# Norm factors worked out on token columns, and two weight tiles taken together while the input is made

## What is computed

```
def rmsnorm(x, g):
    y = x * lax.rsqrt(jnp.mean(x * x, axis=-1, keepdims=True) + RMS_EPS)
    return y * g
def layer_norm(x, g, b):
    mu, var = mean of x, mean of (x - mu)^2 over channels
    return (x - mu) * lax.rsqrt(var + LN_EPS) * g + b
...
    f_l = modulate(rmsnorm(h_lat, norm2[i]), sh2_l, sc2_l)        # x * (1 + scale) + shift
    h_lat = h_lat + g2_l * peer(f_l, peer_wq[i], ...)
    return rmsnorm(h_lat, final_norm)
...
    h_l = xl * (1.0 + sc1_l) + sh1_l                              # second block, layer i
    o_l, o_c = even_mixer(h_l, h_c, ...)                          # i = 0; odd_mixer for i = 1
    xl = layer_norm(ALPHA * xl + gt1_l * o_l, ln1_g[i], ln1_b[i])
    h_l = xl * (1.0 + sc2_l) + sh2_l
    f_l = conv_ffn(h_l, w_gate[i], w_up[i], conv_w[i], conv_b[i], w_down[i])
    xl = layer_norm(ALPHA * xl + gt2_l * f_l, ln2_g[i], ln2_b[i])
```

## Time and profile before

| | us |
|---|---|
| median of 3 runs | 4767.77 (4763.95 to 4772.82) |
| the profiled execution, own time | 4765.72 |
| its span, first to last instruction | 4763.8 |
| TensorE busy | 4363.6 (92%) |
| VectorE busy | 2498.6 (52%) |
| GpSimd busy | 1804.2 (38%) |
| mean granted clock of TensorE | 0.959 |

### The profile page before, as it was taken

One profiled execution on the slowest core, in us unless ns is written; L12 is line 12 of the kernel. 1 busy time (PEld: TensorE's weight loads), 2 busy tenths in 40 slices (PEclk: granted clock), 3 DMA queues, 4 the chain that ended last, 5 costly groups with the idle time before them and its releaser, 6 DMA issues.

```text
span 4763.8 us, 51427 instructions
## 1 busy us (share of the span) xinstructions
PE 4363.6 (92%) x20890; PEld 3398.6 (71%) x20890; DVE 2498.6 (52%) x4227; ACT 1510.1 (32%) x2528; POOL 1804.2 (38%) x987
## 2 busy tenths in 40 slices
PE   7878999987779999999999989997999979988998
PEld 3667755456667888888888866675888857656886
DVE  4675745359868676664544342544344350364334
ACT  3212211034863232323222233543222232353232
POOL 2244423024965444444444413002223315333442
PEclk9998999989889999999999989998999989998999
DMA  5200300321355555454533310001212112102331
GB/s 216 81 27 6 117 27 27 133 85 49 128 199 187 171 172 173 155 177 163 181 129 133 116 62 15 19 19 40 67 63 67 63 31 62 36 1 71 97 93 49
DMA packets 170761, 441.31 MB, mean 93 GB/s; under 512 B 12220, under 2 KB 78972, under 8 KB 167581
## 3 DMA queue, kind: packets, MB, share of 16 engines
q1 hardware_dynamic: 168060, 422.61, 26.1%
q0 software_dynamic: 2464, 15.41, 0.8%
HBM read 402.32 MB, written 35.65 MB: 92 GB/s over the span
## 4 chain that ended last, share of the span: by engine, by line
PE 69%; DVE 6%; POOL 4%; ACT 3%; issue 2%; DMA 0%; POOLq 0%; ACTq 0%; DVEq 0%
PE psum L256 19%; PE psum L254 19%; PE psum L255 19%; PE psum L260 11%; POOL o L1600 2%; PE psum L281 1%; DVE o L1493 1%; POOL Pe L2411 1%; POOL Pd L2413 1%; DVE X L1882 1%; DVE ffl L1822 0%; DVE o L1495 0%; DVE rstd L1862 0%; DVE X L1885 0%; DVE ci L1444 0%
## 5 line engine op out<-in xcount | busy, mean ns | idle before, releaser
L244 POOL TENSOR_TENSOR pair<-raw_ring,pair 128x1024 fp32r<-128x1024 f32 x502 | 1244.4, 2493 | 2010.6 <-ACT pair L236 2010.5
L236 ACT CAST pair<-raw_ring 128x1024 fp32r<-128x1024 f32 x502 | 510.9, 1047 | 368.8 <-PE psum L256 315.7
L254 PE MATMUL psum<-pfh,pair 128*128 128x512 f32 x1152 | 451.6, 392 | 27.6 <-POOL pair L244 26.8
L1675 DVE SCALAR_TENSOR_TENSOR h<-psum,mods,h 128x512 f32<-128x512 f32 x512 | 370.7, 748 | 162.5 <-PE psum L256 160.7
L255 PE MATMUL psum<-pfl,pair 128*128 128x512 f32 x1152 | 449.9, 391 | 0.0
L256 PE MATMUL psum<-pfh,pair 128*128 128x512 f32 x1152 | 449.7, 390 | 0.0
L254 PE MATMUL psum<-ffh,pair 128*128 128x512 f32 (+1 forms) x1056 | 375.8, 356 | 44.9 <-DVE ffl L1822 44.9
L254 PE MATMUL psum<-Ah,pair 128*128 128x512 f32 x1024 | 400.9, 391 | 9.7 <-DVE h L1675 4.9
L255 PE MATMUL psum<-Al,pair 128*128 128x512 f32 x1024 | 400.5, 391 | 0.0
L256 PE MATMUL psum<-Ah,pair 128*128 128x512 f32 x1024 | 400.3, 391 | 0.0
L256 PE MATMUL psum<-ffh,pair 128*128 128x512 f32 (+1 forms) x1056 | 377.7, 358 | 0.0
(11 more groups left out here) (569 smaller groups left out, 8959.6 us busy)
## 6 DMA issues: line engine op xcount, KB each, us to landing
raw_ring<-wmod SPq DMA_DIRECT2D x144, 512.0 KB, 4.7
raw_ring<-peeru SPq DMA_DIRECT2D x128, 512.0 KB, 4.4
raw_ring<-peerv SPq DMA_DIRECT2D x128, 512.0 KB, 3.7
gates<-stage SPq DMA_DIRECT2D x16, 2048.0 KB, 6.4
Gb<-gates SPq DMA_DIRECT2D x32, 1024.0 KB, 9.5
raw_ring<-win SPq DMA_DIRECT2D x48, 512.0 KB, 4.5
raw_ring<-wgate SPq DMA_DIRECT2D x44, 512.0 KB, 3.5
raw_ring<-wup SPq DMA_DIRECT2D x44, 512.0 KB, 3.6
```

Source lines behind the costliest of these rows:

```text
L236: ac.e.copy(self.pair(t)[0], k.R.of(t)).then_inc(*k.A.up("hi", t))
L244: po.e.tensor_tensor(lo, k.R.of(t), hi.bitcast(F), ALU.subtract).then_inc(*k.G.up("lo", t))
L254: e.matmul(out, w[0], x[0], start=first, stop=False, skip_group_check=True)
L1675: e.scalar_tensor_tensor(out=h[:, j, :], in0=B.of(("down", gi, j)), scalar=m[:, 40 + j, 0:1], in1=h[:, j, :], op0=ALU.mult, op1=ALU.add).t ...
```

## The change

1. **Token columns.** The sum over channels is made with the data as the stationary side and one moving column, so that 128 tokens land on 128 partitions in one PSUM column (`tensor_columns`): 12 such matmuls for an RMS norm, 6 or 4 for a layer norm. Eps, root and reciprocal are then taken of a tile of 128x4 or 128x6 (`vector_column`, `scalar_column`), and `tensor_along` spreads the factor over all partitions with the identity as moving side (`rb`, one PSUM bank for each segment).
2. **Gain and modulation put together.** gain x (1 + scale) and bias x (1 + scale) + shift are made ahead of time (`vector_gains`). VectorE multiplies by gain and by the factor straight from PSUM, ScalarE adds the bias and rounds to the high part in one instruction, VectorE makes the low part of (x + bias) - high. Tiles 2 and 5 (`SECONDS`) have their low part made on GpSimd, from a copy with the bias that ScalarE writes.
3. **The residual** for the next layer is made behind the input, by `vector_keep`, from a copy of the factor in SBUF; it replaces the multiplication by ALPHA.
4. **Sums on GpSimd.** For norm2 and n3 ScalarE squares each h tile as it is made and GpSimd adds tiles 0 to 5 (`pool_squares`). For the means GpSimd adds X tiles 0 to 5 (`pool_sum`), so three products stand in place of eight, all behind the last projection.
5. **The variance's matmuls** are 64 output rows wide, in halves of the bank by turns, with four buffers for squares; a column of ones at rows 0 and 64 (`sel`) adds the halves in step 1. ScalarE copies the sums out of PSUM for it.
6. **Two weight tiles together.** `project_abreast` takes the first two weight tiles of a stage (wq 0 and 1, abin 0 and 1, gate 0 and up 0, dqk 0 and 1): for each input tile it multiplies both. It waits for both tiles' splits and for all of their banks ahead of the first matmul. The scores of wq 0 and 1 both come behind wq 2, the rotations of dqk 0 and 1 behind both.
7. Small things: the weights' first splits stand ahead of the norm at norm2 and n3 (and GpSimd's at the others, ahead of tiles 2 and 5), two small instructions on `mods` stand ahead of the last h, the context's load is issued earlier, the last norm writes the output with one VectorE and one ScalarE instruction a tile.

```diff
+def project_abreast(k, pe, names, x, segs, each, among=(0, 1, 2, 3, 4, 5, 6, 7)):
+    for n in names:
+        pe.wait_ge(k.W.split(n))
+        for s in range(len(segs)):
+            k.B.take((n, s), 1, among)
+            pe.wait_ge(k.B.free((n, s)))
+    for q in range(8):
+        qs = slice(128 * q, 128 * q + 128)
+        pe.wait_ge(each(q))
+        for n in names:
+            hi, lo = k.W.pair(n)
+            for s, (a, b) in enumerate(segs):
+                i = trio(pe.e, k.B.of((n, s))[:, 0:b - a], (hi[:, qs], lo[:, qs]), x(q, s), q == 0, q == 7)
+                if q == 7:
+                    i.then_inc(*k.P.up(n, s))
+    for n in names:
+        k.P.name("used", n)
...
+SECONDS = (2, 5)
+def second_made(k, key, q):
+    return k.G.at(key, "f", q) if q in SECONDS else k.V.at(key, "f", q)
+def pool_seconds(k, po, key, n, tmp, fh, fl):
+    for j in SECONDS:
+        po.wait_ge(k.A.at(key, "g", j))
+        po.e.tensor_tensor(fl[j][:, 0:n], tmp[j % len(tmp)][:, 0:n], fh[j][:, 0:n].bitcast(F), ALU.subtract).then_inc(*k.G.up(key, "f", j))
...
+def tensor_columns(k, pe, key, sources, n, w, among=(0, 1, 2, 3, 4, 5, 6, 7)):
+    bank = k.B.take((key, "col"), 1, among)
+    pe.wait_ge(k.B.free((key, "col")))
+    for i2, (x, ready) in enumerate(sources):
+        for c in range(n):
+            pe.wait_ge(ready(c))
+            i = mm(pe.e, bank[:, c:c + 1], x[:, 128 * c:128 * c + 128], w, i2 == 0 and c == 0, i2 == len(sources) - 1)
+    i.then_inc(*k.P.up(key, "col"))
...
+def tensor_along(k, pe, key, segs, among=(0, 1, 2, 3, 4, 5, 6, 7)):
+    for s in range(len(segs)):
+        k.B.take((key, "rb", s), 1, among)
+        pe.wait_ge(k.B.free((key, "rb", s)))
+    for s, (a, b) in enumerate(segs):
+        bank = k.B.of((key, "rb", s))
+        pe.wait_ge(k.V.at(key, "r"))
+        for c in range(a // 128, b // 128):
+            i = mm(pe.e, bank[:, 128 * c - a:128 * c - a + 128], k.r8[:, c:c + 1].to_broadcast([128, 128]), k.sq["ident"])
+        i.then_inc(*k.P.up(key, "rb", s))
...
+def vector_column(k, dv, key, n, eps):
+    r = k.r8[:, 0:n]
+    dv.wait_ge(k.P.at(key, "col"))
+    dv.e.tensor_scalar(r, k.B.of((key, "col"))[:, 0:n], eps, None, ALU.add).then_inc(*k.V.up(key, "ms"))
+    k.B.over((key, "col"), k.V.now())
+    dv.wait_ge(k.A.at(key, "sqrt"))
+    dv.e.reciprocal(r, r).then_inc(*k.V.up(key, "r"))
...
+    pool_squares(k, po, "sq2", k.psum, k.psq)
     k.G.name("end", "out")
+def pool_squares(k, po, key, total, sq):
+    for j in range(1, 6):
+        po.wait_ge(k.A.at(key, j))
+        po.e.tensor_tensor(total, sq[0] if j == 1 else total, sq[j % 4], ALU.add).then_inc(*k.G.up(key, j))
+        po.wait_ge(k.G.now())
...
-    everyone(k, pe, "out")
-    bank = B.take("ms2")
-    pe.wait_ge(B.free("ms2"))
-    for j in range(8):
-        pe.wait_ge(A.at("sq2", j))
-        mm(e, bank, k.sq["m1024"], k.psq[j % 2], j == 0, j == 7).then_inc(*P.up("sq2", j))
+    tensor_columns(k, pe, "n2", squares(k, "sq2", k.psum, k.psq), 4, k.sq["m1024"][:, 0:1])
+    tensor_along(k, pe, "n2", SEG1)
     P.name("end", "norm2")
-    everyone(k, pe, "norm2")
...
-    for n in range(16):
+    project_abreast(k, pe, [("wq", n) for n in range(2)], k.px, SEG1, lambda q: second_made(k, "n2", q))
+    for n in range(2, 16):
         project(k, pe, ("wq", n), k.px, SEG1)
-        if n:
-            scores(n - 1)
+        if n == 2:
+            scores(0)
+        scores(n - 1)
...
+    W.hi(ac, ("wq", 0))
+    scalar_column(k, ac, "n2", 4)
...
+    W.lo(po, ("wq", 0))
+    pool_seconds(k, po, "n2", 512, k.pft, k.pfh, k.pfl)
...
+def vector_apply(k, dv, key, src, segs, tmp, fh, fl):
...
+    for j in range(10):
+        if j < 8:
+            x = tmp[j % 4]
+            dv.wait_ge(second_made(k, key, j - 4) if j > 3 else None)
+            for s, (a, b) in enumerate(segs):
+                dv.wait_ge(k.P.at(src, "rb", s))
+                e.scalar_tensor_tensor(out=x[:, a:b], in0=k.X[:, j, a:b], scalar=c.gain[s][:, j:j + 1], in1=k.B.of((src, "rb", s))[:, 0:b - a],
+                                       op0=ALU.mult, op1=ALU.mult).then_inc(*V.up())
+                if j == 7:
+                    k.B.over((src, "rb", s), V.now())
+            V.name(key, "x", j)
+        i = j - 2
+        if i < 0 or i in SECONDS:
+            continue
+        dv.wait_ge(k.A.at(key, "hi", i))
+        for s, (a, b) in enumerate(segs):
+            e.scalar_tensor_tensor(out=fl[i][:, a:b], in0=tmp[i % 4][:, a:b], scalar=c.bias[s][:, i:i + 1], in1=fh[i][:, a:b].bitcast(F),
+                                   op0=ALU.add, op1=ALU.subtract).then_inc(*V.up())
+        V.name(key, "f", i)
...
+def scalar_apply(k, ac, key, src, segs, tmp, fh):
+    e, A, c = ac.e, k.A, k.lnv[key]
     for j in range(8):
-        x = tmp[j % 2][:, 0:n]
-        ac.wait_ge(ready(j), k.V.at(key, "f", j - 2) if j > 1 else None)
+        x = tmp[j % 4]
+        ac.wait_ge(k.V.at(key, "x", j))
         for s, (a, b) in enumerate(segs):
-            e.activation(x[:, a:b], k.X[:, j, a:b], AF.Identity, scale=k.ones16[:, 8 * s + j:8 * s + j + 1], bias=m[:, j0 + j, s:s + 1]).then_inc(*A.up())
-        A.name(key, "x", j)
-        ac.wait_ge(A.now())
-        e.copy(fh[j][:, 0:n], x).then_inc(*A.up(key, "hi", j))
-def vector_affine(k, dv, key, segs, tmp, fh, fl):
-    n = segs[-1][1]
+            e.activation(fh[j][:, a:b], x[:, a:b], AF.Identity, bias=c.bias[s][:, j:j + 1]).then_inc(*A.up())
+        A.name(key, "hi", j)
+        if j in SECONDS:
+            ac.wait_ge(A.now())
+            for s, (a, b) in enumerate(segs):
+                e.activation(x[:, a:b], x[:, a:b], AF.Identity, bias=c.bias[s][:, j:j + 1]).then_inc(*A.up())
+            A.name(key, "g", j)
+    for s, (a, b) in enumerate(segs):
+        e.copy(k.rstd[:, a:b], k.B.of((src, "rb", s))[:, 0:b - a]).then_inc(*A.up(key, "rstd", s))
+        k.B.over((src, "rb", s), A.now())
...
+def vector_keep(k, dv, key, n):
+    e, V, c = dv.e, k.V, k.lnv[key]
+    dv.wait_ge(k.A.at(key, "rstd", (n - 1) // 512), V.now())
     for j in range(8):
...
+        x = k.X[:, j, 0:n]
+        e.scalar_tensor_tensor(out=x, in0=x, scalar=c.ga[:, j:j + 1], in1=k.rstd[:, 0:n], op0=ALU.mult, op1=ALU.mult).then_inc(*V.up())
+    dv.wait_ge(V.now())
+    for j in range(8):
+        x = k.X[:, j, 0:n]
+        e.tensor_scalar(x, x, c.ba[:, j:j + 1], None, ALU.add).then_inc(*V.up())
...
         bank = k.B.of((key, "mean", s))
-        pe.wait_ge(count(s), k.B.free((key, "mean", s)) if j == 0 else None)
-        i = mm(pe.e, bank[:, 0:b - a], k.sq["m1024"], k.X[:, j, a:b], j == 0, j == 7)
+        pe.wait_ge(ready(s), k.B.free((key, "mean", s)) if j == 5 else None)
+        x = total[:, a:b] if j == 5 else k.X[:, j, a:b]
+        i = mm(pe.e, bank[:, 0:b - a], k.sq["m1024"], x, j == 5, j == 7)
...
+    for s in range(len(segs)):
         k.B.take((key, "var", s), 1, SIX)
         pe.wait_ge(k.B.free((key, "var", s)))
     for j in range(8):
         pe.wait_ge(k.A.at(key, "sq", j))
         for s, (a, b) in enumerate(segs):
-            i = mm(pe.e, k.B.of((key, "var", s))[:, 0:b - a], k.sq["m1024"], sqt[j % 2][:, a:b], j == 0, j == 7)
+            h = slice(64 * ((j + s) % 2), 64 * ((j + s) % 2) + 64)
+            i = mm(pe.e, k.B.of((key, "var", s))[h, 0:b - a], k.sq["m1024"][:, 0:64], sqt[j % 4][:, a:b], j < 2, j > 5)
         i.then_inc(*k.P.up(key, "var", j))
-def vector_norm(k, dv, key, segs, last=None):
+    n = segs[-1][1] // 128
+    tensor_columns(k, pe, key, [(total, lambda c: k.A.at(key, "sums", c // 4))], n, k.sel, SIX)
+    tensor_along(k, pe, key, segs, SIX)
...
+    vector_column(k, dv, key, segs[-1][1] // 128, LN_EPS)
...
     for s, (a, b) in enumerate(segs):
-        ac.wait_ge(k.V.at(key, "var", s))
-        e.activation(k.rstd[:, a:b], k.rstd[:, a:b], AF.Sqrt).then_inc(*A.up(key, "sqrt", s))
...
+        ac.wait_ge(k.P.at(key, "var", 7))
+        e.copy(total[:, a:b], k.B.of((key, "var", s))[:, 0:b - a]).then_inc(*A.up(key, "sums", s))
+        k.B.over((key, "var", s), A.now())
+    scalar_column(k, ac, key, n // 128)
...
-        if j:
-            tensor_mean(k, pe, key, j - 1, segs, lambda s: k.V.at(key, "res", j - 1, s))
-    tensor_mean(k, pe, key, 7, segs, lambda s: k.V.at(key, "res", 7, s))
-    tensor_norm(k, pe, key, segs, sqt)
+    tensor_mean(k, pe, key, 5, segs, total, lambda s: k.G.at(key, "sum", 5))
+    for j in (6, 7):
+        tensor_mean(k, pe, key, j, segs, total, lambda s: k.V.at(key, "res", j, s))
...
-            project_in(k, pe, ("gate", i, j), fx, segs, None if j else (lambda q: V.at(key, "f", q)), EIGHT)
+            if j == 0:
+                project_abreast(k, pe, [("gate", i, j), ("up", i, j)], fx, segs, lambda q: second_made(k, key, q))
+                continue
+            project_in(k, pe, ("gate", i, j), fx, segs, None, EIGHT)
...
-    vector_affine_scale(k, dv, key, m, 24, segs, A.at("end", before))
```

(11 more changed lines are left out.)

313 lines of the change are left out of this document (179 added, 134 removed).

## The result

| | before | after |
|---|---|---|
| median | 4770.3 (4763.95 to 4777.06, 4 runs) | 4697.1 (4690.99 to 4698.38, 4 runs) |
| span of the profiled execution | 4763.8 | 4695.3 |
| TensorE busy | 4363.6 | 4353.1 |
| mean granted clock | 0.959 | 0.965 |

The ratio is 0.9844, with a 95% interval of 0.9827 to 0.9861. The change is faster by 73 us where I had forecast 111, and the time lies 2 us above the high end of my range, 4695. The spans differ by 68.5 us, so 42.5 us of the forecast are missing.

A forecast was written before the change was run, and what follows sets the result against it. TensorE, busy 92% of the span, was taken as the bound, losing time at six norm-to-projection places. Gains 19.6 + 20.1 + 16.1 + 29 + 16.9 + 9.3 = 111.0 us gave a median of 4657, range 4632 to 4695.

The forecast's parts named there:

- 5 res1, ff1: From res1's norm to ff1's second weight tile: first matmul 4347.9 against 4360.2, end 4361.5 against 4378.4; gain 16.9 us.
- 6 end: From ff1 through the last norm to the output: mean 4.4 us sooner, end 4754.5 against 4763.8; gain 9.3 us.
- B: Rival: the clock stays at 1.2 GHz through the two-tile stretches; +42 us, 4699; chance 14%, whole or in part.
- A: Rival: the variance's 64-row products don't pair, so it costs as many matmul slots as before; +10.6 us, 4668; chance 12%.
- C: Rival: VectorE and GpSimd contend at every place, two to three us each; +13 us, 4670; chance 14%.
- Place 4: From ff0's norm to dqk: no bank collision, kept residual costs nothing; rotation ends 3897.6 against 3926.8; gain 29 us, the largest.
- Place 2: From n3 to abin, the even block's input: first matmul 2794.6 against 2805.74, end 2813.4 against 2833.6; gain 20.1 us.
- Place 3: From res0 to ff0: TensorE waits for a bank the spread factor holds; gain 16.1 us, 28 without that wait.
- place 1: From norm2 to wq, the routing product: TensorE starts about 983.4, end 996.7 against 1016.3; gain 19.6 us.
- D: Rival: the bank wait at res0 to ff0 costs nothing, since the input ends last anyway; 12.7 us less, 4644; chance 12%.
- E: Rival: slower than before, with 1.2 GHz far into the dense projections; 239 us at the low clock eat the gain; 2%.
- F: Rival: the first weight tiles' splits arrive late, so the two tiles aren't abreast; about +33 us, 4690; chance 3%.

## Why the prediction was wrong

The missing 42.5 us, by the steps of the prediction. "Measured" is what each place gained between the work ahead of it and the end of its second weight tile, for places 2 and 4 the start of the third, since the small products of both tiles now lie between.

| place | forecast | measured | what failed |
|---|---|---|---|
| 1 norm2, wq | 19.6 | 20.3 | |
| 2 n3, abin | 20.1 | 13.9 | first matmul 2.5 later; both tiles' small products together, 3.2 |
| 3 res0, ff0 | 16.1 | 14.9 | size only |
| 4 ff0, dqk | 29 | 22.1 | the cover of the kept residual |
| 5 res1, ff1 | 16.9 | 16.0 | size only |
| 6 end | 9.3 | 10.6 | |
| dense stretches | 0 | -32 | no term for it |
| elsewhere | 0 | +3 | 2.9 before norm2; not looked into |

**The sum treated everything outside the six places as unchanged.** That is the step that failed most, three quarters of the gap. The matmuls were the same instructions in the same order, the diff didn't touch them, and I took their duration over from before. What moved them was the allocation of 64 and 576 bytes ahead of them. The shifted versions of both kernels show this, at +30 and -32 us (by spans -28). It accounts for 25 of the 31.8; most of the rest, 6.6, is ff0's 256-column matmuls, at 117.8 ns for 113.3, and that cause is open. The trace of before held a hint: the two blocks stand at different remainders there, and their matmuls start 226.7 and 228.9 ns apart. I hadn't compared them. In the range no case had a loss outside the places, so the time fell 2 us above its end. The high bound was also lower than its own cases add up to: B alone is 4657 + 42 = 4699, and A, C and half of B are 4702, where I wrote 4695. With these it would have held the time, but not by its mechanism: the largest loss is in none of its cases.

**Place 4, the residual: "lies behind ff0's first two tiles ... nothing".** I had costed this for ff0 and then took it for dqk too. At ff0, TensorE has 96 matmuls ahead that ask VectorE for nothing. At dqk the next thing is a rotation that wants ScalarE, which wants two tiny products of VectorE that stand behind the residual. My sentence on the cover that could fail (7 us at places 3 and 4) had the size and half of the place: 8.07 us at place 4, none at place 3. Moving the residual gave back 9.4, and 7 in the end.

**Place 2: first matmul at 12.5 us after the last h.** It came after 15.05. I had taken "VectorE now also makes the affine part" as a cost per tile, and not read that three of them, and six products, stand ahead of the first low part in its order, nor that GpSimd's low part of tile 2 collides with it (2.18 for 0.94). The other order gave back 3.4 to 4.2. The second tile's end is 3.1 us later than forecast, so at the forecast's own mark the place gained 17.1. Another 3.2 go before the third tile starts, seen in the trace and not tried by itself: TensorE waits 2.82 us for the copies and squares of both abin tiles, 1.34 before, and its eight products of squares then take 1.7 us longer, at a granted clock of 0.59 (windows 2809.9 to 2814.1), where before it was 1.00.

**Place 3 was right in its mechanism.** The bank wait is there, named by the copy as said, and 34.4 us behind the mean's end for 33.8. Both tiles end at 53.9 for 52.9. The mean came 6.2 us sooner (70.7 us from the first projection of res0 for 76.9), for 6.4. That the wait costs 12 us (28 for 16.1) was right too: with other banks 12.0 came back.

**The steps on token columns held**: the factor, the small root and reciprocal, the spread. At place 1 the first matmul came at 979.96 for 983.4, of which 2.9 us had been gained ahead of the place.

The rivals. **A**, the 64-row products don't pair: no; taking the pairs away costs 11 us. **B**, the clock stays low: a part. Here are place 1, 2, 3 and 4 in the table of windows of after (length, busy us of TensorE, weight loads, VectorE, ScalarE, GpSimd, granted clock, DMA share, GB/s). A mean granted clock of 0.85 amounts to 1.2 GHz for three tenths of the stretch and 2.4 for the rest, and 0.72 to more than half of it.

```profile
979.96:993.10 13.14, 13.14 (x49) 10.65 (x50) 7.76 (x10) 4.93 (x8) 3.41 (x3) 0.85 0.17 55
2787.77:2807.10 19.33, 19.33 (x96) 16.63 (x96) 10.95 (x17) 4.67 (x8) 3.46 (x3) 0.86 0.23 83
3271.70:3291.20 19.50, 19.47 (x96) 16.96 (x97) 12.92 (x19) 1.27 (x4) 0.28 (x1) 0.85 0.00 1
3852.00:3868.60 16.60, 15.49 (x48) 11.39 (x48) 16.36 (x25) 9.91 (x18) 4.29 (x2) 0.72 0.11 33
```

Before, the stretch behind the gap at place 2 had 0.50. **C**, VectorE and GpSimd hinder each other: yes, at every place, but without GpSimd's share the time is the same, so its price beyond what was counted can't be told from nothing. **D**, the bank wait costs nothing: no. **E** and **F** didn't happen; the splits were in time. What I called "something unseen of smaller size" was the largest term of all.

## What to carry to other kernels

Whoever adds a small tile to a kernel that is bound by TensorE should look where all later tiles then lie, and compare a stretch of matmuls that the diff doesn't touch before anything else: here 64 and 576 bytes cost 28 to 32 us of 4700. A step that is put "behind" something must be followed to the first instruction that waits for the engine it stands on, at each place where it occurs. Where banks or buffers are handed out in turn, a shift at one place is a shift at all later ones, and a two-tile projection that asks for all banks at once makes each collision a full wait.

## What the hardware showed unexpectedly

- The start address of the moving data changes the rate of float32 matmuls of 512 columns at full clock: 226.7 ns from one start to the next at remainder 128 of 256 bytes, 228.9 at 192, 232.4 at 0, 233.3 at 64, in ff1. The weight tiles lie at the same addresses in all these kernels, so it isn't they. The experts show the same for 128, 192 and 0.
- 256-column matmuls in ff0 start 113.3 to 119.4 ns apart in different kernels with the same instructions. After had 117.8 at 64 and at 192 and 119.4 at 128; before had 113.3 at 192 and 113.7 at 64, and a kernel in which only bank numbers differ from after had 113.8 at 64. At 128 three different first banks all gave 119.4. The cause stays open.
- Two products of 64 output rows in two halves of a bank, with different moving data, run in pairs: 32 of them take 7.5 us and are held by VectorE, where 128 rows wide they take 10.6.
